# An output stage that scales and turns three row tiles itself, and a last doubling level in quarter tiles

## What is computed

```python
# first block, its end
out = (uf - mu) * lax.rsqrt(var + NORM_EPS) * g + b            # layer norm of every row
# second block, its start
hdn = rms_norm_2(x, norm_g[i]) * (1.0 + scale) + shift         # rms norm, then a modulation
y = gated_deltanet(hdn, ...)
# inside gated_deltanet, for 16 heads x 4 chunks of 128 rows
l_mat = a_mat + eye                                            # unit lower triangular, 128 x 128
t_mat = lax.linalg.triangular_solve(l_mat, eye, left_side=True, lower=True, unit_diagonal=True)
u = t_mat @ (v * beta);  w = t_mat @ (kb * exp(gc))
def step(state, inp):                                          # chunk after chunk
    v_new = uc - wc @ state
    o = qd @ state + qkc @ v_new
    state = state * gl + kd.T @ v_new
```

## Time and profile before

| | us |
|---|---|
| median of 3 runs | 1125.43 (1124.95 to 1127.58) |
| the profiled execution, its whole time | 1124.68 |
| its span, first to last instruction | 1122.9 |
| TensorE busy | 1070.3 (95%) |
| VectorE busy | 680.2 (61%) |
| ScalarE busy | 446.3 (40%) |
| GpSimd busy | 235.3 (21%) |
| mean granted clock of TensorE | 0.986 of full |

### The profile page before, as it was taken

How to read it: one execution, slowest core, us unless ns; L and a number is a source line. 1 busy time by engine, 2 the same in 40 slices (tenths; PEclk the granted TensorE clock), 3 DMA queues, 4 the chain that set the end, 5 groups by cost and what they waited for, 6 DMA issues and landing times. The chain is left out here.

```text
span 1122.9 us, 14447 instructions
## 1 busy us (share of the span) xinstructions
PE 1070.3 (95%) x5558; PEld 889.2 (79%) x5558; DVE 680.2 (61%) x1132; ACT 446.3 (40%) x821; POOL 235.3 (21%) x167
## 2 busy tenths in 40 slices
PE   7999999999899999999799999999999986999997
PEld 4888888888688877788678788888878975889886
DVE  4245426632166678546836756667875669976635
ACT  4223214333256553141423333367525456325432
POOL 0001000000000143001100100004204756245792
PEclk9999999999999899989999999999999999999999
DMA  8276534332121222032333445343212211203501
GB/s 295 86 265 230 186 113 133 111 96 72 61 100 48 98 97 75 1 132 76 129 107 113 150 150 188 113 164 117 94 57 94 92 61 57 75 19 100 183 1 75
DMA packets 58305, 123.95 MB, mean 110 GB/s; under 512 B 5760, under 2 KB 5888, under 8 KB 58112
## 3 DMA queue, kind: packets, MB, share of 16 engines
q1 hardware_dynamic: 55792, 110.22, 29.0%
q0 software_dynamic: 2304, 12.58, 3.2%
q10 hardware_dynamic: 144, 0.26, 0.1%
HBM read 108.90 MB, written 14.16 MB: 110 GB/s over the span
## 5 line engine op out<-in xcount | busy, mean ns | idle before, releaser
L287 DVE TENSOR_TENSOR w_lo<-raw,w_hi 128x2048 fp32r<-128x2048 f32 x58 | 135.1, 2329 | 213.8 <-ACT w_hi L283 207.1
L283 ACT ACTIVATE w_hi<-raw 128x2048 fp32r<-128x2048 f32 x51 | 97.6, 1913 | 222.4 <-PE projections_ps L131 138.3
L129 PE MATMUL projections_ps<-projections_x_hi,w_hi 128*128 128x512 f32 x208 | 81.1, 390 | 0.4 <-ACTq L503 0.4
L130 PE MATMUL projections_ps<-projections_x_lo,w_hi 128*128 128x512 f32 x208 | 80.9, 389 | 0.0
L131 PE MATMUL projections_ps<-projections_x_hi,w_lo 128*128 128x512 f32 x208 | 80.9, 389 | 0.0
L129 PE MATMUL projections_ps<-w_hi,projections_x_hi 128*128 128x512 f32 x192 | 74.7, 389 | 0.0
L130 PE MATMUL projections_ps<-w_lo,projections_x_hi 128*128 128x512 f32 x192 | 74.7, 389 | 0.0
L131 PE MATMUL projections_ps<-w_hi,projections_x_lo 128*128 128x512 f32 x192 | 74.7, 389 | 0.0
L244 DVE SCALAR_TENSOR_TENSOR resid<-resid,mixer_cw 128x512 f32<-128x512 f32 x96 | 64.9, 746 | 0.0
L2405 POOL TENSOR_TENSOR mixer_es<-masks,mixer_gsel 128x1024 f32<-128x1024 f32 x8 | 18.3, 2293 | 213.1 <-PE mixer_ps L1875 134.1
L129 PE MATMUL output_ps<-w_hi,output_m_hi 128*128 128x512 f32 x128 | 54.1, 423 | 1.1 <-DVE output_m_lo L1246 0.7
(11 more groups left out here) (319 smaller groups left out, 2641.8 us busy)
## 6 DMA issues: line engine op xcount, KB each, us to landing
raw<-in_w_in SPq DMA_DIRECT2D x26, 1024.0 KB, 5.0
raw<-in_gdn_w_in SPq DMA_DIRECT2D x24, 1024.0 KB, 5.1
tok<-in_ada_w POOLq DMA_DIRECT2D x16, 768.0 KB, 6.2
raw<-in_w_out SPq DMA_DIRECT2D x8, 1024.0 KB, 5.0
qkv_kept<-mixer_ring SPq DMA_DIRECT2D x8, 1024.0 KB, 4.2
mixer_st<-qkv_kept SPq DMA_DIRECT2D x32, 256.0 KB, 2.9
raw<-in_gdn_w_out SPq DMA_DIRECT2D x8, 1024.0 KB, 5.6
resid<-in_att_bias SPq DMA_DIRECT2D x16, 256.0 KB, 2.8
```

The source lines that it names most:

```text
L129: nc.tensor.matmul(out, w_hi, x_hi, start=first, stop=False, skip_group_check=True)
L130: nc.tensor.matmul(out, w_hi, x_lo, start=False, stop=False, skip_group_check=True)
L283: self.nc.scalar.activation(self.hi[s][:], self.raw[s][:], ACT.Copy).then_inc(self.hi_ready, 1)
L287: engine.tensor_tensor(self.lo[s][:], self.raw[s][:], self.hi[s][:], ALU.subtract)\
```

## The change

In the passage VectorE waits for the norm's factor ahead of both of its products (`layer_norm`); the scaling of the rows 0 to 2 goes from VectorE to ScalarE (behind the next row's squares); GpSimd makes the norm's factor of the next tile ahead of the second factor of this one; the modulation's sum goes to bank 0; TensorE turns the row tiles 0 to 2 of the first four column tiles ahead of the barrier, and only the fourth behind it; the other four column tiles are turned in the midst of the first products. For this the PSUM tensor `ps` is made once and handed to both functions. In the heads all of level 1 works on quarters: V1 takes the 64 x 64 block of `C` and of `T` into the lower 64 partitions, Z1 takes those back to the upper ones, T turns 64 x 64, the copies of V and T on ScalarE move 64 partitions by 256, and the masked write of Z1 on VectorE becomes a plain copy of 64 partitions by 256. The second level mask goes.

```diff
@@ scan_and_output, TensorE @@
-            pe.wait_ge(added, GROUPS + 1)
+            pe.wait_ge(added, GROUPS + TT + 1)
             for j in range(3 * KT):
-                mm = nc.tensor.matmul(ps[:, 4, j:j + P], mod_acc[:, j * P:(j + 1) * P], ones, start=True, stop=True)
+                mm = nc.tensor.matmul(ps[:, 0, j:j + P], mod_acc[:, j * P:(j + 1) * P], ones, start=True, stop=True)
             mm.then_inc(mod_sum, 1)
+            for t in range(TT - 1):
+                pe.wait_ge(next_ok, t + 1)
+                for e in range(4):
+                    tr = nc.tensor.transpose(ps[:, 4 + e, t * P:(t + 1) * P], tok[:, t, e * P:(e + 1) * P], ident)
+            tr.then_inc(next_turned, 1)
@@ ScalarE @@
+                if t:
+                    act.wait_ge(factor_ok, ROW_FACTOR[t - 1])
+                    nc.scalar.activation(tok[:, t - 1, 0:D_MODEL], resid[:, t - 1, :], ACT.Copy, scale=row_f[:, t - 1:t])\
+                        .then_inc(next_ok, 1)
@@ GpSimd @@
+            layer_factor(0)
             for t in range(TT):
-                layer_factor(t)
+                if t + 1 < TT:
+                    layer_factor(t + 1)
                 last_factor(t)
@@ VectorE @@
-                dve.wait_ge(var_ok, t + 1)
+                dve.wait_ge(factor_ok, LAYER_FACTOR[t])
                 own.did(nc.vector.scalar_tensor_tensor(out=resid[:, t, :], in0=resid[:, t, :],
                                                        scalar=mean_var[:, t, 0:1], in1=row_g[:],
                                                        op0=ALU.subtract, op1=ALU.mult))
-                return own.n
-            def after_factor(t, step):
-                dve.wait_ge(factor_ok, 2 * t + 3)
-                own.wait(step)
+                own.wait()
                 nc.vector.scalar_tensor_tensor(out=resid[:, t, :], in0=resid[:, t, :], scalar=ln_f[:, t:t + 1],
                                                in1=row_b[:], op0=ALU.mult, op1=ALU.add).then_inc(normed, 1)
...
-                    nc.vector.tensor_scalar(tok[:, t - 1, 0:D_MODEL], resid[:, t - 1, :], row_f[:, t - 1:t], None, ALU.mult)
@@ second_mixer, TensorE, start @@
+            def turn_x(e):
+                if e >= 4:
+                    pe.wait_ge(h_ok, e - 3)
+                for t in range(TT - 1 if e < 4 else 0, TT):
+                    tr = nc.tensor.transpose(ps[:, 4 + e % 4, t * P:(t + 1) * P], xn[:, t, e * P:(e + 1) * P], ident)
+                tr.then_inc(h_turned, 1)
+            pe.wait_ge(xn_ok, 1)
+            for e in range(4):
+                turn_x(e)
...
                         if e == 0:
+                            if s == 0:
+                                turn_x(4 + kk)
                             pe.wait_ge(low_ok, k + 1)
@@ doubling, TensorE @@
+                    if lv and kind == "V":
+                        mm = nc.tensor.matmul(out[LOW, 0:64], C[UP, 8 * j + m, 64:P], T[UP, m, 0:64], start=True, stop=True)
+                    elif lv:
+                        mm = nc.tensor.matmul(out[UP, 64:P], V[LOW, m, 0:64], U[j % 2][LOW, m, 64:P], start=True, stop=True)
...
-                        mm = nc.tensor.transpose(out, U[j % 2][:, m, :], ident)
+                        mm = nc.tensor.transpose(out[UP, 0:64], U[j % 2][UP, m, 0:64], ident[UP, 0:64])
@@ ScalarE @@
+                    if lv:
+                        nc.scalar.activation(V[LOW, ms4, 0:64], src[LOW, :, 0:64], ACT.Copy).then_inc(v_out, 1)
...
-                    nc.scalar.activation(T[:, ms4, :], src, ACT.Copy).then_inc(t_out, 1)
+                    nc.scalar.activation(T[UP, ms4, 0:64], src[UP, :, 0:64], ACT.Copy).then_inc(t_out, 1)
@@ VectorE @@
+                    if lv:
+                        nc.vector.tensor_copy(U[j % 2][UP, 4 * grp:4 * grp + 4, 64:P],
+                                              psZ[UP, grp, :].rearrange("p (m c) -> p m c", c=P)[:, :, 64:P]).then_inc(u_ok2, 1)
+                        return
```

More of the change, by code:

```diff
@@ L66, in block_masks @@
     j, l = np.arange(P)[:, None], np.arange(P)[None, :]
[L67 removed]
+    levels = [(j // (2 * b) == l // (2 * b)) & (j // b < l // b) for b in (32,)]
     return np.stack([j < l, j // 32 == l // 32] + levels, 1).astype(np.float32)
@@ L858, in _, with scan_and_output @@
                     exponentials(a_next, TILES[3:])
-def scan_and_output(nc, a, ahead, wba, wba_in, mix_in, split, raw, att_f, m_g, masks, small, resid, row_f, tok, xbc, dt, adt, modc,
+def scan_and_output(nc, a, ps, ahead, wba, wba_in, mix_in, split, raw, att_f, m_g, masks, small, resid, row_f, tok, xbc, dt, adt, modc,
                     g_col, gain):
@@ L1404, in _, with second_mixer @@
                                            op0=ALU.add, op1=ALU.mult)
-def second_mixer(nc, a, ahead, wba, wba_in, split, raw, masks, resid, row_f, modc, gain, small, z):
+def second_mixer(nc, a, ps, ahead, wba, wba_in, split, raw, masks, resid, row_f, modc, gain, small, z):
     w_in = a["gdn_w_in"][0].rearrange("(k p) c -> p k c", p=P)
```

32 lines of the change are left out of this document (14 added, 18 removed).

## The result

The changed kernel's median is 1119.88 us (20 runs, 1114.63 to 1123.7), that of the kernel before on the same chip 1126.95 (20 runs, 1120.78 to 1127.59). The ratio is 0.995, its 95% interval 0.9934 to 0.9967: 3.7 to 7.4 us faster, where 12.1 were forecast and the range ended at 1119. The profiled execution took 1114.79 (span 1113.0), which is near the lowest of its 20; that of before took 1124.68. Two single traces are thus no measure of the change. Of the 20 runs of the changed kernel the mean granted clock is 0.986 in those at 1114.6 to 1115.3, 0.981 in those at 1119, and 0.977 in those from 1123.0 to 1123.7. Their time follows their clock. Both traces of the changed kernel (this one and that of `after_again`, at 1114.95) are of executions near the fast end, so no trace shows where an execution at 1119 to 1124 stands at the lower clock.

What follows compares the result with a forecast made beforehand. TensorE, working for 95% of the span, was taken as the bound. Heads 10.8 and passage 1.3 sum to 12.1 off 1124.68, giving 1112.6; the median's 0.75 on top makes 1113.3 us, range 1110 to 1119.

Steps and rivals of the forecast that it cites:

- The mechanism in the heads: In the doubling and head loops, TensorE's unhidden fills get shorter with quarter tiles: 5.4 us per half, 10.8 in all.
- the wait of 0.41 for the copy: At a head loop's end, TensorE's wait of 0.41 us for VectorE's masked copy was to go.
- a doubling: Ahead of the head loops, the doubling of pair 0 running alone was to lose 1.66 of its 11.30 us.
- the loops j = 2: Last head loop of each half: gain of 0.95 us, as the turning of output doesn't wait for the copy.
- T's shape: Quarter-size T transposes: a slot from 0.44 to 0.25 us, gaining nothing in the loops and 0.19 in a doubling.
- VectorE's new wait: In the passage, VectorE waits 0.95 to 1.0 us for the factor ahead of both products; worth next to nothing itself.
- The small instruction: A quarter product in the heads was put at 0.0625 us, range 0.055 to 0.111; a V or Z slot at 0.50.
- the wait for VectorE's w_sb ahead of O: In the head loops, O was to wait for VectorE's w_sb, starting at 885.51 instead of 886.39.
- the walk: One head loop followed step by step: next values' transposes start 1.4 us earlier for j = 0 and 1.
- The half-way case of the first rival: In the heads, entering and leaving small shapes costs 0.09 each: 0.7 off each loop's gain, 1117.5 us; inside the 0.75 case.
- The passage's clock: TensorE's granted clock in the passage, 0.67 from 545 to 550 before; 1.5 us kept for either outcome.
- The third rival: In the head loops the granted clock falls over quarter products: 36 us over six loops, about 1149; chance 0.04.

Runs made afterwards that it cites:

- after_again: The changed kernel, unchanged, run and traced a second time against the kernel before: median 1121.28 us (12 runs), ratio 0.9962.
- before_again: The kernel before, unchanged, run and traced a second time: median 1126.91 us (12 runs).
- the passage alone: The kernel before with only the passage's part of the change, the doubling as before: median 1129.11 us (12 runs), ratio 1.0019.

## Why the prediction was half right

**Right.** The mechanism in the heads: the fills were TensorE's path, the wait of 0.41 for the copy went but for 0.1, the small instructions start 0.058 apart (0.06 said), a doubling fell by 2.0 (1.66 said), the loops j = 2 by 1.5 and 0.55 (0.95 each said), T's shape gains nothing. Cleanly, from traces without half level, the heads are worth 2.0 + 2.0 for the doublings, 0.89 x 4 for loops, and 1.5 + 0.55: 9.6 of the 10.8. The traces of `before_again` and `after_again`, with no half level in a doubling or first loop, differ by the same 9.6 behind the passage. The doubling came near by luck: its copies gave 0.46 (0.69 said), T 0.05 (0.19 said), and the products of V1 and Z1 1.5 (0.78 said), because all sixteen instructions of each stand on that chain (1.14 instead of 1.85 from V1's first to Z1's first) and the prediction counted eight. In the passage, the barrier came 0.56 later (0.6 said), the first product 15.3 behind the sum (15.0 said), and the whole 27.5 at full clock (27.6 said); VectorE's new wait was worth next to nothing (a row tile every 5.19 us instead of 5.35).

**The terms that were mis-sized.** The small instruction was put at 0.0625 in a slot that pays nothing at its ends. Its own 0.058 was near that, but a slot took 0.61 and not 0.50, since 0.14 falls on its first and last spacing, and the full products beside it paid 0.10 more on entering and 0.10 on leaving. So TensorE stayed the one that sets the pace (16.46 of 16.50 us), and the wait for VectorE's w_sb ahead of O, which the walk had as the next limit and as a sign to look for, didn't come. The half-way case of the first rival had just this (0.18 on four slots, 0.7 a loop), and the trace has 0.69. I had the row (0.32 instead of 0.23 ahead of the 32 x 32 transposes) and left it out of the sum. The Trainium skill's sentence, in "TensorEngine Tiling (Array Packing)", Key Properties, that changing the tiling mode drains TensorE, was the rule to follow. This case's runs agree that a change of shape costs time, about 0.33 a slot in all (0.10 + 0.10 in the neighbours and 0.14 in the slot); that it is a drain no row shows. A loop so gained 0.89, not 1.4.

**The step that failed.** The passage's clock: the sum took 1.3 at full clock and left the clock to the bounds ("I keep 1.5 us for either outcome"). The old passage didn't feel its half level, which ended ahead of its first product; the new one starts its products earlier and so runs the first of them at half level. That stretch was also never short with the new order: 6.8 us in both traces of the whole change and 10.2 in that of the passage alone, where the old passage had 3.4 in four traces and 6.8 in two. The passage gains 0.2 to 0.3 or loses 1.2, where +1.3 was said. The same step failed behind the doublings, where the sum had nothing for the clock, as the next paragraph tells.

**The third rival, in small.** It had the clock falling behind quarter products, for six loops at 36 us, at a chance of 4%. It did not come from the loops, where TensorE is busy all the time (16.46 of 16.50), but began at the end of the doublings that run alone (7.92 busy of 9.30) and ran into the loop behind, for 3.4 to 6.8 us at a time. It took 1.4 to 2.7 us in 7 of 16 cases: 1.7 x 2 x 7/16 = 1.5 a run on average. That is an estimate from eight traces.

The sum as the runs have it: heads 9.6, passage 0.2 to -1.2, half level behind doublings -1.5 on average: 6.9 to 8.3, against 7.1 between the two medians of the first comparison and 4.3 to 5.6 by the two ratios. With the 0.2 of the whole change's own traces the sum is 8.3, and what remains to the measured gains, 1 to 4 us, I can't place. Half level also strikes at 930 to 959, between the halves, once or twice in a trace in every kernel (1.7 or 3.4 us of work lost). Whether the change shifts its odds can't be told from so few traces, and no execution of the whole change above 1115 was traced. And the forecast was laid on a single pair of numbers (1124.68 and 1125.43 of three runs), where the kernel before ranges over 6.8 us and has its middle at 1126.9. Of the 6.6 us between the forecast of 1113.3 and the measured 1119.88 this starting point is 1.5; the rest is the gain, 7.1 instead of 12.1.

## What to carry to other kernels

Price a small tile with its two neighbours: a shape that differs from theirs cost 0.33 us a slot here, 0.14 on entering and 0.19 on leaving, of which 0.1 each falls on the neighbour. So make few long runs of small tiles rather than many short ones. When a change makes TensorE the one that sets the pace in a stretch, ask at which clock it runs there: half level that cost nothing before is then paid for, and where there is time to spare, keep the work in one piece or fill the wait with products that nothing reads. Judge by medians over many runs and by stage times of traces, never by the difference of two spans.

## What the runs showed that I had not expected

One version beats both kernels: the quarter tiles, all transposes behind the barrier, and the fill (1113.3 and 1115.4 in its two comparisons, ratios 0.9898 and 0.9925). The interval of the second, 0.9899 to 0.9952, still overlaps that of the change. The same wait doesn't always bring the same clock: with 2.3 us of idle time near 473 us TensorE fell to half level in 18 of 20 traces, for 6.8 or 10.2 us in which it soon was busy without a gap, and in two it didn't. Time at half level and time lost are two things: the old passage at a clock of 0.88, 0.94 and 1.00 took the same 28.8 to 28.9 us. And a product with 64 moving columns and full weights costs 0.105 an instruction against 0.111 for 128 columns.
